# First feed-forward chunk of each layer in two halves of rows, with the first norm and the p projection interleaved

## Chip, cores and metric

One core of a Trainium2 chip runs the whole program in one launch. The metric is the device time of that core in microseconds; the kernel before has a median of 2168.04 us over 3 runs (2167.68 to 2173.33).

## What is computed

The reference is a stack of two blocks over 256 positions of width 1024, in float32. The first block (two layers with attention, memory attention and a gated scan) is not touched. The second has four layers, and each is, cut to what matters:

```python
for i in range(DEPTH_2):                       # 4 layers
    h = mixer_i(x)                             # gla, mla, conv, gla; ends in a product with w_out
    x = layer_norm(ALPHA * x + h, ln_g[i, 0], ln_b[i, 0])                       # first norm
    x = layer_norm(ALPHA * x + sq_relu_mlp(x, mlp_w1[i], mlp_w2[i]), ln_g[i, 1], ln_b[i, 1])
    x = x + jax.nn.sigmoid(x @ ple_w_gate[i]) * (p[i] @ ple_w_proj[i])
```

The feed-forward part squares relu(x @ w1), with w1 of 1024 x 4096, and multiplies with w2, 4096 x 1024. Its hidden width goes in 8 chunks of 512. The projection p @ ple_w_proj (256 x 1024) needs nothing of x.

## The kernel before, in words

`plan()` writes out one list of steps by hand, and every engine walks that same list in order, taking from each step its own part and meeting the others at semaphores. So the list's order is each engine's own order of work.

Weights come as units of 128 x 2048 floats (1 MB), numbered in order of use. SP loads unit n into slot n % 4 of `raw` once the low part of unit n - 4 is made (L746 to L751). ScalarE makes the high part `whi` (`hi`, L1125 to L1130) once the unit that held that slot is done with, told by `unit_begun`; the rest `wlo = raw - whi` is made by VectorE (`lo`, L1427 to L1430) or, for the feed-forward units, by GpSimd (L757 to L767). The step `ahead` and the flag `ahead` of a step say where in the list this is done, three units ahead for ScalarE and two for VectorE. Activations are split in the same way, into `XTh`, `XTl` for X and `YTh`, `YTl` for Y, after being turned (transposed) by TensorE in tiles of 128 x 128; a step `turn` takes 128 rows (h) and 512 columns (c): four transposes (L959), ScalarE's copy to the high part (L1245), VectorE's subtraction for the low part (L1882). Each product is three matmuls, high by high, high by low and low by high (`passes`, L786 to L794, the matmul on L789).

`wait_turned` (L776) makes TensorE wait until what was turned into X or Y is there; a turn marked late counts only for a step that asks for the whole. A turn of p goes to "E", a part of the Y buffers, and L965 and L966 let it count for Y too.

Around the change a layer goes (L441 to L470): the product with w_out in two single units and a tail of two (`output_pair`, which finishes the four quarters, 128 rows by 512 columns each, one after the other), with p turned ahead of the tail. Then the p projection in two halves of columns (`lattm`, 12 matmuls of 512 columns in each half). Then the first norm, `ln` steps on VectorE (L2050 to L2100): for each quarter the sum with the residual (L2057) and statistics (L2061), after two quarters of the same rows the "rest": mean and variance, the normalising products (L2079), an inverse square root by three Newton steps (L2090, L2093), gain and bias into `xres` (L2098). Then the turns of X, rows 0 to 127 first, and chunk 0 of the feed-forward part in two units (u), 512 rows of w1 each. There and in all of `project_unit` in this form the weights are stationary and 256 positions stream: `o` covers all 256 columns of half a bank. The step `mlp` does the other chunks in a loop; its first is chunk 1 (L1104). GpSimd makes the low parts of all 32 feed-forward units of a layer in a loop, each as soon as its high part is there.

Of the kernel before, what the change touches and what calls it, by code (L numbers as in the profile page):

```python
# [24 lines left out]
P = 128  # L25
# [22 lines left out]
def plan():  # L48
# [21 lines left out]
    def add(step, **f):  # L70
        steps.append((step, f))
# [49 lines left out]
    def flush():  # L121
        while late:
            late.pop(0)()
# [97 lines left out]
    def layer_norm(g, early):  # L221

        for c in range(2):
            add("ln", g=g, h=0, part=c)
        add("ln", g=g, h=0, part="rest")
        add("ln", g=g, h=1, part=0)
        if early:
            for c in range(2):
                turn("x", 0, c, "X", 4 * c)
        add("ln", g=g, h=1, part=1)  # L230
        add("ln", g=g, h=1, part="rest")
        if not early:
            for c in range(2):
                turn("x", 0, c, "X", 4 * c)

# [196 lines left out]
    for i in range(LAYERS2):  # L432
# [12 lines left out]
        for b in range(2):  # L445
            if b == 0:
                unit("lattm", (("ple_w_proj", i), "K", 0, 0), g=pg, b=0, k=8)
            else:
                add("lattm", n=len(units) - 1, g=pg + 1, b=1, k=8)
            add("post", g=pg + b, tag="ple", b=b, on="sv")  # L450
        if i == 2:
            add("load", what="gla1")
        layer_norm(q, early=False)
        turn("x", 1, 0, "X", 0)
        turn("x", 1, 1, "X", 4, late=True)
        n0, g = len(units), n["p"]
        unit("proj", ("mlp1", i, 0, 0), g=g, u=0, src="X", fm=True)
        flush()
        add("loadln", i=i, k=1)
        unit("proj", ("mlp1", i, 1, 0), g=g, u=1, src="X", fm=True)  # L460
        add("mlp", i=i, n=n0, g=g, q=n["q"])
        for c in range(1, FF_CHUNKS):
# [140 lines left out]
def build(nc, a, steps, units, heads, totals):  # L603
    NU = len(units)
    with ExitStack() as ctx:
# [151 lines left out]
        @block.gpsimd  # L757
        def _(pool):
            def lo(n, slot):
                pool.wait_ge(hi_done, n + 1)  # L760
                pool.tensor_tensor(wlo[:, slot, :], raw[:, slot, :], whi[:, slot, :],  # L761
                                   ALU.subtract).then_inc(lo_pool, 1)

            for first in (f["n"] for kind, f in steps if kind == "mlp"):
                with pool.Fori(0, 4 * FF_CHUNKS // RING) as i:
                    for s in range(RING):
                        lo(i * RING + (first + s), (first + s) % RING)  # L767
# [3 lines left out]
        def _(pe):  # L771
# [24 lines left out]
            def project_unit(n, slot, g, u, fm, XH=XTh, XL=XTl, KH=4, kx=0, pool_less=None):  # L796
# [8 lines left out]
                for b in range(2):  # L805
# [17 lines left out]
                    elif u == 1:  # L823
                        mm.then_inc(p_done[1], 1)
                return mm

            def output_pair(n, slot, work, XH, XL, k0, first=False):
# [104 lines left out]
            for kind, f in steps:  # L932
                if kind == "turn":
# [29 lines left out]
                    else:  # L963
                        ready[f["dst"]] = f["t"] + 1
                    if f["dst"] == "E":  # L965
                        ready["Y"] = f["t"] + 1  # L966
                elif kind == "proj":
                    wait_turned("Y" if f["src"] == "M" else "X", whole=f["u"] == 1)
                    xs = (YTh, YTl) if f["src"] == "M" else (XTh, XTl)
                    project_unit(f["n"], f["n"] % RING, f["g"], f["u"], f["fm"], *xs)  # L970
                elif kind == "out":
                    wait_turned("Y" if f["src"] == "Y" else "X", whole=False)
# [93 lines left out]
                elif kind in ("latfm", "lattm"):  # L1066
                    wait_turned("Y")
                    wait_lo(pe, f["n"])
# [47 lines left out]
        def _(act):  # L1116
# [96 lines left out]
            for kind, f in steps:  # L1213
# [46 lines left out]
                elif kind in ("latfm", "lattm"):  # L1260
                    if f["b"] == 0:
                        ahead(f["n"])
# [155 lines left out]
        def _(dve):  # L1418
# [393 lines left out]
            for kind, f in steps:  # L1812
# [60 lines left out]
                elif kind in ("latfm", "lattm"):  # L1873
                    if f["b"] == 0:
                        ahead(f["n"])
# [287 lines left out]
```

## Time and profile before

| | |
|---|---|
| median of 3 runs | 2168.04 us |
| the profiled execution | 2167.73 us, of it the span 2165.9 us |
| TensorE busy | 1956.8 us (90%) in 11184 matmuls |
| VectorE busy | 1255.8 us (58%) |
| ScalarE busy | 903.6 us (42%) |
| GpSimd busy | 592.2 us (27%) in 132 instructions |
| DMA | 324.95 MB, mean 150 GB/s |
| mean granted clock of TensorE | 0.962 of 2.4 GHz |

Engines are PE (TensorE matmul), PEld (its weight loads, which overlap), DVE (VectorE), ACT (ScalarE), POOL (GpSimd) and SP. Matmuls are pipelined, so one's duration holds a latency and the pace of a run of them is read from their starts. "L789" is a line of the kernel. A row's bracket says how long the engine was idle ahead of it and who ended that.

### The profile page before, as it was taken

Reading aid. Unit: us, or ns where it says so; the run is one execution under the profiler, and the core shown is the slowest. Engines: PE = TensorE matmul, PEld = TensorE weight load, DVE = VectorE, ACT = ScalarE, POOL = GpSimd, SP = SyncE. Lnnn points to the kernel's source line nnn. Section 1 sums busy time; section 2 is a strip of 40 time slices with the busy share of each in tenths; the row PEclk is TensorE's granted clock in tenths of the full one; section 3 lists DMA queues with packets and bytes.
Section 4 is the critical chain, followed back from the end, with each engine's and each line's share of the span. In section 5 each row is a group of like instructions: output and inputs, shape, how many; then the busy total and the mean of one; then the engine's idle time right before and its main releaser. Section 6 shows DMA issues by size and latency. Waiting matters only on the chain.

```text
span 2165.9 us, 27617 instructions
## 1 busy us (share of the span) xinstructions
PE 1956.8 (90%) x11184; PEld 1710.1 (79%) x11184; DVE 1255.8 (58%) x2094; ACT 903.6 (42%) x969; POOL 592.2 (27%) x132
## 2 busy tenths in 40 slices
PE   6999999899988888999977899989899989879998
PEld 4878877678876776899765699979799977769996
DVE  7777787776876487332764533265732375873235
ACT  4544444345342333344343344434344434334442
POOL 0000000000000002678100378700278700027870
PEclk9999999999899999999999899989999999989999
DMA  6434333533232224455431445534545533254551
GB/s 260 159 127 156 138 135 124 202 146 127 79 136 99 101 94 160 164 187 194 165 117 39 163 174 195 183 142 177 191 166 194 194 117 136 78 180 175 185 195 47
DMA packets 53109, 324.95 MB, mean 150 GB/s; under 512 B 8432, under 2 KB 11888, under 8 KB 15760
## 3 DMA queue, kind: packets, MB, share of 16 engines
q1 hardware_dynamic: 43024, 308.38, 38.6%
q10 hardware_dynamic: 9984, 15.17, 2.2%
q8 instruction: 71, 1.16, 0.2%
q14 instruction: 30, 0.25, 0.0%
HBM read 322.47 MB, written 1.05 MB: 149 GB/s over the span
## 4 chain that ended last, share of the span: by engine, by line
PE 68%; DVE 25%; ACT 3%; issue 3%; DMA 1%; SPq 0%; DVEq 0%; ACTq 0%
PE project L789 37%; PE output L789 24%; DVE wlo L1430 4%; DVE tok L2079 2%; DVE arena L1533 1%; DVE arena L1801 1%; DVE XTl L1882 1%; PE turn L959 1%; PE output L904 1%; PE output L926 1%; DVE xres L2098 1%; DVE st L2061 1%; DVE tok L2057 1%; ACT whi L1130 1%; DVE st L1524 1%
## 5 line engine op out<-in xcount | busy, mean ns | idle before, releaser
L761 POOL TENSOR_TENSOR wlo<-raw,whi 128x2048 fp32r<-128x2048 f32 x128 | 592.0, 4651 | 1524.6 <-ACT whi L1130 1524.2
L1130 ACT ACTIVATE whi<-raw 128x2048 fp32r<-128x2048 f32 x291 | 554.3, 1913 | 511.8 <-PE project L789 311.5
L789 PE MATMUL project<-XTh,whi 128*128 128x256 f32 x1488 | 429.5, 289 | 9.7 <-DVE XTl L1882 8.7
L789 PE MATMUL project<-XTh,wlo 128*128 128x256 f32 x1488 | 427.2, 287 | 0.0
L789 PE MATMUL project<-XTl,whi 128*128 128x256 f32 x1488 | 426.9, 287 | 0.0
L1430 DVE TENSOR_TENSOR wlo<-raw,whi 128x2048 fp32r<-128x2048 f32 x163 | 376.2, 2321 | 66.6 <-ACT whi L1130 66.3
L2107 DVE TENSOR_TENSOR arena<-arena 128x512 f32<-128x512 f32 x64 | 142.4, 2259 | 463.1 <-ACT arena L1380 463.1
L789 PE MATMUL output<-whi,YTh 128*128 128x512 f32 x736 | 293.3, 398 | 21.1 <-DVE YTl L1882 16.7
L789 PEld LDWEIGHTS project<-XTh,whi 128*128 128x128 f32 x1488 | 292.3, 196 | 13.7 <-DVE XTl L1882 11.5
L789 PEld LDWEIGHTS project<-XTh,wlo 128*128 128x128 f32 x1488 | 292.2, 196 | 1.0
L789 PEld LDWEIGHTS project<-XTl,whi 128*128 128x128 f32 x1488 | 291.9, 196 | 0.0
L789 PE MATMUL output<-wlo,YTh 128*128 128x512 f32 x736 | 291.1, 396 | 0.0
L789 PE MATMUL output<-whi,YTl 128*128 128x512 f32 x736 | 290.5, 395 | 0.0
L789 PE MATMUL project<-whi,XTh 128*128 128x512 f32 x624 | 256.6, 411 | 14.4 <-DVE XTl L1882 8.8
L789 PE MATMUL project<-wlo,XTh 128*128 128x512 f32 x624 | 246.6, 395 | 0.0
L789 PE MATMUL project<-whi,XTl 128*128 128x512 f32 x624 | 246.2, 395 | 0.0
L789 PEld LDWEIGHTS output<-whi,YTh 128*128 128x128 f32 x736 | 141.3, 192 | 52.3 <-DVE YTl L1882 18.3
L789 PEld LDWEIGHTS output<-whi,YTl 128*128 128x128 f32 x736 | 140.8, 191 | 30.3
L789 PEld LDWEIGHTS output<-wlo,YTh 128*128 128x128 f32 x736 | 141.1, 192 | 28.0
L789 PEld LDWEIGHTS project<-whi,XTh 128*128 128x128 f32 x624 | 119.7, 192 | 42.2 <-DVE XTl L1882 9.7
L789 PEld LDWEIGHTS project<-whi,XTl 128*128 128x128 f32 x624 | 119.3, 191 | 26.2
L789 PEld LDWEIGHTS project<-wlo,XTh 128*128 128x128 f32 x624 | 119.7, 192 | 23.7
(225 smaller groups left out, 2187.6 us busy)
## 6 DMA issues: line engine op xcount, KB each, us to landing
raw<-in_units SPq DMA_DIRECT2D x291, 1024.0 KB, 4.8
arena<-in_ln_g ACTq DMA_DIRECT2D x8, 512.0 KB, 3.9
arena<-in_ln_b ACTq DMA_DIRECT2D x8, 512.0 KB, 4.8
tok<-in_mem SPq DMA_DIRECT2D x2, 512.0 KB, 5.9
arena<-in_mem_norm_gain ACTq DMA_DIRECT2D x2, 512.0 KB, 4.9
arena<-in_norm_gain ACTq DMA_DIRECT2D x2, 512.0 KB, 5.5
xres<-in_x SPq DMA_DIRECT2D x1, 1024.0 KB, 14.9
arena<-in_mem ACTq DMA_DIRECT2D x1, 1024.0 KB, 7.3
```

The costliest lines, as they stand in the source:

```text
L761: pool.tensor_tensor(wlo[:, slot, :], raw[:, slot, :], whi[:, slot, :], ALU.subtract).then_inc(lo_pool, 1)
L789: mm = pe.matmul(out, x if x_stationary else w, w if x_stationary else x, start=start and i == 0, stop=stop and i == 2, skip_group_check=True)
L904: mm = pe.matmul(PQ[h2][:, h * S:(h + 1) * S], qkT[:, h2, h * P:(h + 1) * P], qkT[:, h2, S:2 * S], start=True, stop=True)
L926: mm = pe.matmul(PQ[3][:, h * P:(h + 1) * P], pT[:, h2, kt * S + h * P:kt * S + (h + 1) * P], v, start=kt == 0, stop=kt == 1)
L959: mm = pe.transpose(PT[f["t"] % 2][:, x * P:(x + 1) * P], s, ident[:, :])
L1130: act.activation(whi[:, slot, :], raw[:, slot, :], ACT.Copy).then_inc(hi_done, 1)
L1430: dve.tensor_tensor(wlo[:, slot, :], raw[:, slot, :], whi[:, slot, :], ALU.subtract).then_inc(lo_dve, 1)
L1524: dve.tensor_reduce(st[:, 16 + 4 * b:20 + 4 * b], sq[:, b, :].rearrange("p (j d) -> p j d", j=4), AX_X, ALU.add).then_inc(dve_own, 1)
L1533: ins = dve.scalar_tensor_tensor(out=v, in0=v, scalar=st[:, 24 + x:25 + x], in1=gain, op0=ALU.mult, op1=ALU.mult)
L1801: ins = dve.copy_predicated(dst, m, src)
L2079: first = [lambda c=c: dve.scalar_tensor_tensor(out=tok[:, h, c * 512:(c + 1) * 512], in0=tok[:, h, c * 512:(c + 1) * 512], scalar=mean, i ...
L2107: dve.tensor_tensor(hsq[:, b, :], relu[:, b, :], relu[:, b, :], ALU.mult).then_inc(hsq_ready, 1)
```

## The change

Around the first norm, the p projection's first half stays ahead of the norm's steps; the turns of rows 0 to 127 come before the second half, and the rest of the norm of rows 128 to 255 comes behind it in the list. A turn into "E" no longer counts for Y, and the p projection waits for "E". Chunk 0 is no longer two `proj` steps but two `first` steps, with new code (`first_chunk`): step h=0 multiplies both units with positions 0 to 127, then rows 128 to 255 are turned, and step h=1 multiplies the same two units with positions 128 to 255. GpSimd's loop has its first four units written out, the third of which waits until the first norm has written all of `xres`. The high parts of the third feed-forward unit and the fourth are made later in the list.

```diff
--- before.py
+++ after.py
@@ -224,14 +224,13 @@
             add("ln", g=g, h=0, part=c)
         add("ln", g=g, h=0, part="rest")
         add("ln", g=g, h=1, part=0)
+        if not early:
+            add("ln", g=g, h=1, part=1)
+        for c in range(2):
+            turn("x", 0, c, "X", 4 * c)
         if early:
-            for c in range(2):
-                turn("x", 0, c, "X", 4 * c)
-        add("ln", g=g, h=1, part=1)
-        add("ln", g=g, h=1, part="rest")
-        if not early:
-            for c in range(2):
-                turn("x", 0, c, "X", 4 * c)
+            add("ln", g=g, h=1, part=1)
+            add("ln", g=g, h=1, part="rest")
 
     def quad(kind, vg, j0=0, **f):
         q = n["quad"]
@@ -444,21 +443,25 @@
         n["p"] += 2
         for b in range(2):
             if b == 0:
-                unit("lattm", (("ple_w_proj", i), "K", 0, 0), g=pg, b=0, k=8)
+                unit("lattm", (("ple_w_proj", i), "K", 0, 0), ahead=False, g=pg, b=0, k=8)
             else:
-                add("lattm", n=len(units) - 1, g=pg + 1, b=1, k=8)
+                layer_norm(q, early=False)
+                add("lattm", n=len(units) - 1, g=pg + 1, b=1, k=8, ahead=False)
             add("post", g=pg + b, tag="ple", b=b, on="sv")
+        add("ln", g=q, h=1, part="rest")
+        add("ahead", n=len(units) - 1)
         if i == 2:
             add("load", what="gla1")
-        layer_norm(q, early=False)
+        n0, g = len(units), n["p"]
+        units.extend(("mlp1", i, u, 0) for u in range(2))
+        add("first", n=n0, g=g, h=0)
+        add("ahead", n=n0)
         turn("x", 1, 0, "X", 0)
-        turn("x", 1, 1, "X", 4, late=True)
-        n0, g = len(units), n["p"]
-        unit("proj", ("mlp1", i, 0, 0), g=g, u=0, src="X", fm=True)
-        flush()
+        turn("x", 1, 1, "X", 4)
         add("loadln", i=i, k=1)
-        unit("proj", ("mlp1", i, 1, 0), g=g, u=1, src="X", fm=True)
-        add("mlp", i=i, n=n0, g=g, q=n["q"])
+        add("first", n=n0, g=g, h=1)
+        add("ahead", n=n0 + 1)
+        add("mlp", i=i, n=n0, g=g, q=n["q"], src_n=n["src"])
         for c in range(1, FF_CHUNKS):
             units.extend(("mlp1", i, u, c) for u in range(2))
             units.extend(("mlp2", i, u, c - 1) for u in range(2))
@@ -761,8 +764,12 @@
                 pool.tensor_tensor(wlo[:, slot, :], raw[:, slot, :], whi[:, slot, :],
                                    ALU.subtract).then_inc(lo_pool, 1)
 
-            for first in (f["n"] for kind, f in steps if kind == "mlp"):
-                with pool.Fori(0, 4 * FF_CHUNKS // RING) as i:
+            for first, normed in ((f["n"], f["src_n"]) for kind, f in steps if kind == "mlp"):
+                for s in range(RING):
+                    if s == 2:
+                        pool.wait_ge(tsrc, normed)
+                    lo(first + s, (first + s) % RING)
+                with pool.Fori(1, 4 * FF_CHUNKS // RING) as i:
                     for s in range(RING):
                         lo(i * RING + (first + s), (first + s) % RING)
 
@@ -823,6 +830,28 @@
                     elif u == 1:
                         mm.then_inc(p_done[1], 1)
                 return mm
+
+            def first_chunk(n, g, h):
+
+                t = slice(h * P, (h + 1) * P)
+                for u in range(2):
+                    slot = (n + u) % RING
+                    if h == 0:
+                        wait_lo(pe, n + u)
+                    begin[0] = u == h
+                    wh = whi[:, slot, :].rearrange("p (k c) -> p k c", k=4)
+                    wl = wlo[:, slot, :].rearrange("p (k c) -> p k c", k=4)
+                    for b in range(2):
+                        if h == 0 and u == 0:
+                            pe.wait_ge(p_evac[b], g)
+                        for m in (2 * b, 2 * b + 1):
+                            o = PP[b][:, (m % 2) * S + h * P:(m % 2) * S + (h + 1) * P]
+                            for k in range(4):
+                                mm = passes(o, XTh[:, 4 * u + k, t], XTl[:, 4 * u + k, t], wh[:, k, m * P:(m + 1) * P],
+                                            wl[:, k, m * P:(m + 1) * P], h == 0 and u == 0 and k == 0 and m % 2 == 0,
+                                            h == 1 and u == 1 and k == 3, x_stationary=False)
+                        if h == 1 and u == 1:
+                            mm.then_inc(p_done[b], 1)
 
             def output_pair(n, slot, work, XH, XL, k0, first=False):
 
@@ -962,12 +991,13 @@
                         late[f["dst"]] = f["t"] + 1
                     else:
                         ready[f["dst"]] = f["t"] + 1
-                    if f["dst"] == "E":
-                        ready["Y"] = f["t"] + 1
                 elif kind == "proj":
                     wait_turned("Y" if f["src"] == "M" else "X", whole=f["u"] == 1)
                     xs = (YTh, YTl) if f["src"] == "M" else (XTh, XTl)
                     project_unit(f["n"], f["n"] % RING, f["g"], f["u"], f["fm"], *xs)
+                elif kind == "first":
+                    wait_turned("X")
+                    first_chunk(f["n"], f["g"], f["h"])
                 elif kind == "out":
                     wait_turned("Y" if f["src"] == "Y" else "X", whole=False)
                     xs = (YTh, YTl) if f["src"] == "Y" else (XTh, XTl)
@@ -1064,7 +1094,7 @@
                                         wl[:, k, b * P:(b + 1) * P], k == 0, k == 7, x_stationary=False)
                         mm.then_inc(p_done[b], 1)
                 elif kind in ("latfm", "lattm"):
-                    wait_turned("Y")
+                    wait_turned("E" if units[f["n"]][0][0] == "ple_w_proj" else "Y")
                     wait_lo(pe, f["n"])
                     begin[0] = f["b"] == 0
                     wh = whi[:, f["n"] % RING, :].rearrange("p (k c) -> p k c", k=2)
@@ -1258,7 +1288,7 @@
                     if f["work"][0][1] == 0:
                         ahead(f["n"] + f["h"])
                 elif kind in ("latfm", "lattm"):
-                    if f["b"] == 0:
+                    if f["b"] == 0 and f["ahead"]:
                         ahead(f["n"])
                 elif kind == "post":
                     if "s" in f["on"]:
@@ -1871,7 +1901,7 @@
                     if f["work"][0][1] == 0:
                         ahead(f["n"] + f["h"])
                 elif kind in ("latfm", "lattm"):
-                    if f["b"] == 0:
+                    if f["b"] == 0 and f["ahead"]:
                         ahead(f["n"])
                 elif kind == "turn":
                     t = f["t"]
```

## Rows read from the trace of the kernel before

**Rows 1.** The page, busy time of one engine and the chain by engine.
```profile
PE 1956.8 (90%) x11184; PEld 1710.1 (79%) x11184; DVE 1255.8 (58%) x2094; ACT 903.6 (42%) x969; POOL 592.2 (27%) x132
...
PE 68%; DVE 25%; ACT 3%; issue 3%; DMA 1%; SPq 0%; DVEq 0%; ACTq 0%
```

**Rows 2.** The chain of waits, 840 to 900 us: start, us, what.
```profile
859.20 7.04 DVE tok L2079 x2
...
869.85 1.10 PE turn L959 x4
...
871.61 0.70 DVE XTl L1882
...
872.35 25.61 PE project L789 x192
```

**Rows 3.** The chain of waits over the whole span, its longest pieces.
```profile
897.97 10.91 PE output L789 x48
908.87 11.51 PE project L789 x96
...
1236.18 24.73 PE project L789 x192
...
1566.69 24.98 PE project L789 x192
...
1947.60 25.59 PE project L789 x192
```

**Rows 4.** Windows: stretch, us, each engine's busy us (instructions), granted clock, DMA share, GB/s.
```profile
855.05:861.49 6.44, 5.85 (x27) 4.53 (x26) 6.27 (x11) 4.42 (x5) 5.32 (x2) 1.00 0.04 17
861.49:872.35 10.86, 2.82 (x17) 2.21 (x14) 9.26 (x13) 2.70 (x5) 4.21 (x1) 0.77 0.53 193
872.35:886.46 14.11, 14.11 (x98) 14.11 (x99) 2.85 (x2) 4.50 (x4) 8.13 (x2) 0.81 0.42 150
```

**Rows 5.** Timeline of PE: start, us, instruction, [idle before <- releaser].
```profile
844.05 0.47 PE L789 MATMUL output<-whi,YTh 128*128 128x512 f32 x1 [1.09 <-DVE YTl L1882]
...
858.52 0.47 PE L789 MATMUL project<-whi,YTh 128*128 128x512 f32 x1 [0.59 <-ACT arena L1139]
...
861.34 1.03 PE L959 MATMUL turn<-ident,xres 128*128 128x128 f32 x8
...
1225.17 1.03 PE L959 MATMUL turn<-ident,xres 128*128 128x128 f32 x8
...
1555.67 1.03 PE L959 MATMUL turn<-ident,xres 128*128 128x128 f32 x8
...
1936.62 1.03 PE L959 MATMUL turn<-ident,xres 128*128 128x128 f32 x8
```

**Rows 6.** Timeline of the other engines in the first layer's stretch.
```profile
843.87 2.28 DVE L1430 TENSOR_TENSOR wlo<-raw,whi 128x2048 fp32r<-128x2048 f32 x1
...
851.75 1.42 DVE L2079 SCALAR_TENSOR_TENSOR tok<-tok,st,arena 128x512 f32<-128x512 f32 x2
...
854.62 1.42 DVE L2098 SCALAR_TENSOR_TENSOR xres<-tok,st,arena 128x512 f32<-128x512 f32 x2
...
856.17 9.52 POOL L761 TENSOR_TENSOR wlo<-raw,whi 128x2048 fp32r<-128x2048 f32 x2 [4.96 <-ACT whi L1130]
...
862.03 1.08 ACT L1245 ACTIVATE XTh<-turn 128x512 fp32r<-128x512 f32 x2
```

**Rows 7.** Groups of weight loads by shape (count, busy us, mean ns), and two pieces of PE's timeline.
```profile
L789 PEld LDWEIGHTS project<-XTh,whi 128*128 128x128 f32 x1488 | 292.3, 196 | 13.7 <-DVE XTl L1882 11.5 <-DVE wlo L1430 1.2
...
L926 PEld LDWEIGHTS output<-arena 128*128 128x128 f32 x256 | 32.1, 191 | 5.8 <-DVE arena L1708 4.7
...
L1046 PEld LDWEIGHTS project<-XTl,arena 128*16 128x16 f32 x32 | 3.1, 97 | 3.8
...
134.77 1.06 PE L926 MATMUL output<-arena 128*128 128x128 f32 x8
...
566.35 2.05 PE L1015 MATMUL output<-arena 128*128 128x128 f32 x16 [0.34 <-DVE arena L1760]
```

## The prediction

> **What bounds the kernel now.** I read the page first: the tensor engine is busy for 90% of the span, and the chain that ended last lies on it for 68% and on the vector engine for 25% [rows 1]. So matmul work moves the time one for one, and so do the places where it waits for the vector engine. The change touches one place, four times: from the tail of a layer's output product, over the first norm, to the first two feed-forward chunks. The chain of waits around it in the first layer [rows 2] shows what to see: after the tail the path leaves the tensor engine for the norm; in the second half's norm two instructions take 7.04 us; then come transposes, one more low part of XT, and 25.61 us of first-layer products. Inside the loop the same 96 products take 11.51 us and 48 of 512 columns take 10.91 us [rows 3]: 119.9 ns and 227.3 ns apart. The 192 products of chunks 0 and 1 should then take 23.02 us; they took 25.61, 24.73, 24.98 and 25.59 us [rows 2, 3]. The windows say why: from 861.49 to 872.35 the tensor engine was busy 2.82 of 10.86 us, and the next 14.11 us ran at a granted clock of 0.81, a mix of 1.2 and 2.4 GHz [rows 4]. The timeline gives the points I count from [rows 5].
>
> **Part 1, the tail no longer waits for the turned p.** In before a turn into "E" also raises what "Y" stands for, so the tail, which reads only Y, waits for p's low part: 1.09 us, ahead of the tail [rows 5], and alike in all four layers. The change takes that line out and lets only the p projection wait. The low part needed next, for the tail's second unit, was made long before; and the tail's end sets the norm's start. Each layer gains 1.09 us. The VectorE subtraction that stood behind p's turn ends at 846.15 [rows 6], about when the tail's first quarter now ends, so some 0.1 us may come back; I leave it out.
>
> **Part 2, the norm and the p projection change places.** The first half of the projection stays ahead; the two turns of rows 0 to 127 and then the second half follow. The turns cost 8 transposes at 0.11 us, 0.9 us (8 took 1.03 with the last one's 0.27 latency [rows 5]), where PE stood 0.59 us waiting for ScalarE's copy (the idle time at 858.52 [rows 5]). That copy was late since ScalarE made two high parts in front of it; one is now deferred. So the second projection ends 0.9 - 0.59, less what was already overlapped, about 0.15 us later; I take 861.40 for the start of the first half-chunk in the old time, against 861.34 for the old turns [rows 5]. Is its input ready? The norm of rows 0 to 127 ends at 854.62 + 1.42 = 856.04 [rows 6], the statistics of the other rows at 859.2, where L2079 began [rows 2]. ScalarE's two copies take 1.08 us [rows 6], the two low parts 0.70 each [rows 2], so XT's first half is whole at about 860.5: in time by 0.9 us, hidden behind the second projection. Without that cover PE would stand from 858.7 to 860.5, 1.8 us.
>
> **Part 3, the stall of the second norm.** L2079 takes 1.42 us for two in the first half's norm [rows 6] and 7.04 us in the second's [rows 2]. GpSimd's low parts of the weights run 856.17 to 865.69 [rows 6], and the pair ended just after: both read two tensors from SBUF. The change holds the third low part back until the norm has written all its rows. The first of these two ends at 860.8, about where the rest of the norm now begins (it stands behind the two low parts of XT), so the norm of rows 128 to 255 should take from its L2079 on what the first took, 851.75 to 856.04 [rows 6]: it ends near 865.1, before the first half-chunk ends. So it leaves the path altogether; even with the whole 5.6 us stall it would end at 870.7, still before about 872.7. What is late next is no norm but the products. Held back: the third low part (about 865.2 to 869.8) and the fourth (to 874.4); they are used at about 887. SP's loads behind them and ScalarE's high parts move with them and have the same slack. The fifth and sixth weight units wait for the unit two before to be begun, about 1 us later than now, and are used after 898. LN constants and the third layer's small loads are issued beside products. All that at nothing.
>
> **Part 4, 96 products of 256 columns become 192 of 128.** Stationary are the weights, so every product needs its own weight load, and those double. No such product is in the trace, so I bound it. From below by columns alone: (227.3 - 119.9) / 256 is 0.42 ns a column, so 119.9 - 53.7 = 66 ns, if the load hides. From above, while loads and clock behave as now, by the 256-column product's 119.9. What the load asks is in the groups of weight loads [rows 7]: loads of 128 columns take 191 (plain fp32) and 196 ns (these), one of 16 takes 97; that is 0.84 ns a column, 107 ns for 128. Two loops of plain fp32 with such loads and 128 columns run 8 in 1.06 us and 16 in 2.05 us; less one latency of 0.28 that is 111 and 118 ns each. So the load, not the columns, should set the pace, and halving the columns saves nearly nothing: I take 118, nearest to the longer of the loops and just under the 119.9 of the same instruction.
>
> The skill has another figure. The Trainium skill ("TensorE: Matmul & The Clock Gate", Back-to-back issue gap) gives a sustained stream of loads and matmuls about 81 ns at 128 columns. By it the 192 products would take an estimated 15.6 us, and the sum would come to some 7 us less a layer. That figure's operands are not these; whether it holds here is the second rival's question.
>
> Between the halves stand two turns. The old ones show their cost: begun 861.34, copied by 863.11 [rows 5, 6], plus one low part of 0.70 [rows 2]: 2.5 us in which PE does 0.9 us of transposes.
>
> **Sum per layer**, from the old turns' start to the end of chunk 1. Before: 36.62, 35.74, 36.00 and 36.57 us (872.35 + 25.61 - 861.34, and so on [rows 2, 3, 5]), mean 36.23. After: 0.06 + 192 x 0.118 + 2.5 + 11.51 for chunk 1 + 0.17 latency = 36.90. That is +0.67, less 1.09 from part 1: -0.42 us; over four layers -1.7 us. With 111 to 120 ns it is -7.1 to -0.2 us. The profiled execution took 2167.73 us (span 2165.9 and 1.8 around), 0.3 under the median of 2168.04; I put the same difference on the median: 2166.3 us.
>
> **Rivals.** One, the clock falls in the pause between the halves. Before, the half-rate stretch behind the norm cost 2.6, 1.7, 2.0 and 2.6 us (above 23.02), 8.8 in all; my sum holds none of it. PE idled 7.5 us at a stretch then and would idle some 1.6 now, and the pause at 858.52 left the clock at 1.00 [rows 4], so I think it stays; if not, -1.7 + 8.8 gives 2175 us. Chance 0.08.
> Two, the weight load hides in the reordering and 128 columns cost 66 ns: 12.7 instead of 22.7 us, 10 us a layer, 2126 us (the norm still ends in time). For it: nothing shows a load setting the pace alone. Against it: the 0.84 ns a column. The skill's figure named above lies between. Chance 0.07.
> Three, on the other side, and with one mechanism: products this narrow lose the one-column-a-cycle rate. A plain fp32 product is two instructions of 111 to 118 ns, so 0.23 us each; if 128 columns of this type run at that rate, the half-chunks take 44.2 us, +21.5 a layer, 2252 us. It decides from about 0.13 us a product on. The same 192 at 1.2 GHz throughout (loads of 213 ns, twice 107) would give 2239. Against: the loads in the 256-column loop show the load time alone explains a floor there. Chance 0.13 for both.
> That the change doesn't do what it says (the stall stays) costs nothing, as part 3 showed, so it is no case of its own.
>
> **How the numbers follow.** The forecast has 0.72. About 0.3%, 6.5 us, is what a measurement of this kernel can tell from no change. Its bounds of -7.1 to -0.2 and about 1 us a layer of doubt on the pause make it 0.14 faster, 0.56 same, 0.02 slower; rival one adds 0.06 slower and 0.02 same; rival two 0.07 faster; rival three 0.13 slower. Sum: 0.21, 0.58, 0.21. The range takes the forecast with its bounds (2157) and rival one (2178 with the same doubt), 0.8 together.
>
> **What the profile after would show.** Tail without the 1.09 us wait; L2079 at 1.42 us for two in both halves; 96 products of 128 columns in 11.3 us twice, 2.5 us apart, from about 860.3 on; their granted clock 1.0; chunk 1 ending within a microsecond of 897. Wrong it would be made by products under 0.1 or over 0.13 us apart, by a clock of 0.5 after the pause, or by a weight unit arriving late at chunk 1.

## The result and the profile after

The changed kernel takes 2196.24 us in the median of 4 runs (2192.84 to 2202.01), the kernel before 2167.97 in runs beside it: the ratio is 1.0136, with an interval of 1.011 to 1.0162. It is slower by some 28 us, and outside the range of the prediction.

The page of the changed kernel: span, busy time by engine, and the chain by engine.

```profile
span 2194.5 us, 28359 instructions
...
PE 2017.6 (92%) x11568; PEld 1774.7 (81%) x11568; DVE 1219.1 (56%) x2094; ACT 903.4 (41%) x969; POOL 591.3 (27%) x132
...
PE 72%; DVE 21%; ACT 3%; issue 2%; DMA 1%; SPq 0%; DVEq 0%; ACTq 0%
```

VectorE's share of the chain fell from 25% [rows 1] to 21%, as it should with the norm out of the way, and TensorE's rose from 68% to 72% of a longer span. The 384 added matmuls are the 96 a layer that the split adds; TensorE's busy time grew by 61 us.

The chain of waits over the whole span, after; the pieces that answer to [rows 2, 3]. A piece of 108 is the last 12 products of the p projection and the first half-chunk of 96; a piece of 192 is the second half-chunk and chunk 1.

```profile
853.00 13.41 PE project L796 x108
...
868.97 33.67 PE project L796 x192
902.64 10.91 PE output L796 x48
913.55 11.51 PE project L796 x96
...
1243.84 32.14 PE project L796 x192
...
1581.02 32.08 PE project L796 x192
...
1968.13 33.68 PE project L796 x192
```

The first half is what was hoped for: 13.41 less 2.72 for the 12 wide products is 10.69 us for 96, 111 ns each. The second half is the same 96 products on other rows, and with chunk 1's 11.5 us it should take some 22.2 us. It takes 32.1 to 33.7, in all four layers. The windows of the first layer show where (stretch, us, busy us and count of each engine, granted clock, DMA share, GB/s):

```profile
861.00:866.25 5.25, 5.25 (x50) 5.25 (x49) 0.00 (x0) 0.00 (x0) 5.25 (x2) 1.00 0.26 78
866.25:868.97 2.72, 1.05 (x10) 0.85 (x10) 1.29 (x2) 1.08 (x2) 1.96 (x1) 1.00 0.75 291
868.97:873.00 4.03, 4.03 (x23) 4.03 (x23) 0.00 (x0) 0.00 (x0) 0.00 (x0) 0.60 1.03 345
873.00:878.00 5.00, 5.00 (x25) 5.00 (x25) 0.00 (x0) 0.00 (x0) 0.00 (x0) 0.50 0.28 115
878.00:888.78 10.78, 10.78 (x53) 10.78 (x52) 1.51 (x1) 2.51 (x2) 4.52 (x1) 0.50 0.20 61
888.78:891.00 2.22, 2.22 (x11) 2.22 (x12) 1.29 (x2) 1.75 (x4) 0.00 (x0) 0.50 0.42 177
891.00:894.00 3.00, 3.00 (x18) 3.00 (x17) 0.69 (x1) 1.80 (x2) 1.12 (x1) 0.56 0.00 0
894.00:902.64 8.64, 8.64 (x74) 8.64 (x73) 2.21 (x1) 2.51 (x2) 7.04 (x2) 1.00 0.33 123
```

The clock is 1.0 through the first half and through the pause, 2.72 us in which TensorE is busy 1.05 and idle 1.67. It falls to 1.2 GHz just after the second half has begun, stays there to its end, and comes back only inside chunk 1, which begins at 888.78 and whose products have 256 columns: 4.9 us into it here, and 2.6, 4.0 and 4.7 us in the other layers. TensorE's timeline shows the moment: products 0.11 us apart, then 0.21.

```profile
869.44 0.28 PE L796 MATMUL project<-XTh,wlo 128*128 128x128 f32 x1
869.55 0.28 PE L796 MATMUL project<-XTl,whi 128*128 128x128 f32 x1
869.66 0.33 PE L796 MATMUL project<-XTh,whi 128*128 128x128 f32 x1
869.79 0.42 PE L796 MATMUL project<-XTh,wlo 128*128 128x128 f32 x1
870.00 0.41 PE L796 MATMUL project<-XTl,whi 128*128 128x128 f32 x1
```

The norm did what was predicted. VectorE's and GpSimd's timeline:

```profile
854.80 1.42 DVE L2109 SCALAR_TENSOR_TENSOR tok<-tok,st,arena 128x512 f32<-128x512 f32 x2
...
850.37 4.62 POOL L764 TENSOR_TENSOR wlo<-raw,whi 128x2048 fp32r<-128x2048 f32 x1 [4.21 <-ACT whi L1160]
859.15 9.07 POOL L764 TENSOR_TENSOR wlo<-raw,whi 128x2048 fp32r<-128x2048 f32 x2 [4.17 <-DVE xres L2128]
```

The pair that took 7.04 us [rows 2] takes 1.42, and GpSimd's third low part starts when the norm has written its last rows.

**The account.** From the tail's first product to the end of chunk 1, by the chain, the four layers took 53.92, 53.03, 53.29 and 53.91 us before and take 64.15, 62.62, 62.60 and 64.20: 39.4 more in all. The low clock is 33.67 - 22.48 = 11.2 us in two layers and 9.6 in the other two, 41.6 together (22.48 is what the piece of 192 takes at full clock in the fifth run below; in the sixth it is 22.24). The rest is the prediction's own +2.7, less 5.0 for a pace of 111 in place of 118 ns. Outside this stretch the tail's shorter wait gives 4.4 back, and 6.4 more, which is what is then left of the difference of the spans, went in stretches that the change doesn't touch: in one the clock happened to be 0.86 before,

```profile
615.00:640.00 25.00, 18.87 (x85) 15.66 (x84) 22.89 (x35) 12.46 (x11) 0.00 (x0) 0.86 0.35 126
```

and 1.00 in the same work after:

```profile
613.00:638.00 25.00, 18.88 (x96) 15.46 (x97) 24.22 (x35) 14.39 (x12) 0.00 (x0) 1.00 0.34 126
```

39.4 - 4.4 - 6.4 = 28.6, the difference of the spans. Outside the four stretches the trace before has 126 us at 1.2 GHz and the one after 112, and at half rate 14 us of it cost about 7 (an estimate), enough for the 6.4.

### The profile page after: what moved, and what is told of

Same layout as the page of the kernel before. It is cut to its first block, busy times and chain, and to the rows that moved or that the text cites. A ratio compares the mean times of both kernels' runs of the same rounds, so it can differ in the third digit from the quotient of the medians.

```text
span 2194.5 us, 28359 instructions
## 1 busy us (share of the span) xinstructions
PE 2017.6 (92%) x11568; PEld 1774.7 (81%) x11568; DVE 1219.1 (56%) x2094; ACT 903.4 (41%) x969; POOL 591.3 (27%) x132
## 3 DMA queue, kind: packets, MB, share of 16 engines
HBM read 322.47 MB, written 1.05 MB: 147 GB/s over the span
## 4 chain that ended last, share of the span: by engine, by line
PE 72%; DVE 21%; ACT 3%; issue 2%; DMA 1%; SPq 0%; DVEq 0%; ACTq 0%
PE project L796 41%; PE output L796 24%; DVE wlo L1460 4%; DVE arena L1563 1%; DVE arena L1831 1%; PE turn L988 1%; DVE XTl L1912 1%; PE output L933 1%; PE output L955 1%; ACT whi L1160 1%; DVE st L1554 1%; DVE arena L1725 1%; PE project L1076 1%; DVE arena L1783 1%; DVE arena L1785 1%
## 5 line engine op out<-in xcount | busy, mean ns | idle before, releaser
L796 PE MATMUL project<-XTh,whi 128*128 128x256 f32 (+1 forms) x1616 | 477.2, 295 | 14.5 <-DVE XTl L1912 13.1
L796 PE MATMUL project<-XTh,wlo 128*128 128x256 f32 (+1 forms) x1616 | 475.8, 294 | 0.0
L796 PE MATMUL project<-XTl,whi 128*128 128x256 f32 (+1 forms) x1616 | 475.7, 294 | 0.0
L2137 DVE TENSOR_TENSOR arena<-arena 128x512 f32<-128x512 f32 x64 | 129.3, 2054 | 510.6 <-ACT arena L1410 510.6
L796 PEld LDWEIGHTS project<-XTh,whi 128*128 128x128 f32 x1616 | 330.9, 205 | 17.8 <-DVE XTl L1912 15.1
L796 PEld LDWEIGHTS project<-XTh,wlo 128*128 128x128 f32 x1616 | 331.1, 205 | 1.2
L796 PEld LDWEIGHTS project<-XTl,whi 128*128 128x128 f32 x1616 | 330.9, 205 | 0.0
```

The costliest lines, as they stand in the source:

```text
L796: mm = pe.matmul(out, x if x_stationary else w, w if x_stationary else x, start=start and i == 0, stop=stop and i == 2, skip_group_check=True)
L2137: dve.tensor_tensor(hsq[:, b, :], relu[:, b, :], relu[:, b, :], ALU.mult).then_inc(hsq_ready, 1)
```

## The experiments

The question left by the traces is what brings the clock down and keeps it down: the pause between the halves, or the narrow products themselves. "Pieces" below are those of the chain that hold chunk 1.

A median holds more than the change. The work ahead of the first layer's turn of p is the same in all these kernels, yet in their profiled executions that turn begins anywhere from 834.95 us (run 1) to 850.26 us (run 7), with 41 to 68 us at 1.2 GHz ahead of it. What such differences don't touch is the stretch from p's turn to the end of chunk 1, summed over the four layers: 220.9 us before and 256.0 in the changed kernel. It is given below where it says more than the median.

**1. No pause.** The turns go between the two units of the first half, and the second of these units doesn't wait for them (that part of the edit is left out here).

```diff
-        add("first", n=n0, g=g, h=0)
+        add("first", n=n0, g=g, h=0, us=(0,))
         add("ahead", n=n0)
         turn("x", 1, 0, "X", 0)
         turn("x", 1, 1, "X", 4)
         add("loadln", i=i, k=1)
-        add("first", n=n0, g=g, h=1)
+        add("first", n=n0, g=g, h=0, us=(1,))
+        add("first", n=n0, g=g, h=1, us=(0, 1))
```

> The turns of rows 128 to 255 are issued between the two units of the first half-chunk, so TensorE has no pause between the halves; all products of the changed kernel are kept. Pause theory (the idle 1.7 us brought the clock down): no fall, both halves at 0.111 us a product, from the first narrow product to the end of chunk 1 about 34 us in place of 46 to 47, near 2147 us. Narrow theory (128-column products do not hold the full clock by themselves): the clock still falls, 10 to 15 us after the first narrow product, and stays low until chunk 1; only the 1.7 us of idling go, near 2189 us.

Measured: 2150.7 us (2139.3 to 2158.5, 6 runs), ratio to the kernel before 0.9928 (0.9907 to 0.9949). In the profiled execution, of 2139.3 us, the clock fell in none of the four layers. The chain (240 are 144 narrow products and chunk 1):

```profile
859.05 27.59 PE project L797 x240
...
1217.62 27.59 PE project L797 x240
```

144 at 111 ns and 11.5 us make 27.5. So 21 us of narrow products, with nothing but the turns in between, did not lower the clock here. The other runs are 11 to 19 us longer, about what one fall or two cost, but they need none: the stretch is 206.7 us, 14.2 less than before, which puts the median near 2154, and 2150.7 was measured. The profiled execution was the fortunate one: it spent 95 us at 1.2 GHz outside its four stretches where the kernel before spent 126. The other five have a mean clock of 0.969 to 0.974 in place of 0.978, so more of them was at 1.2 GHz; where in the program was not recorded.

**2. Narrow products alone.** The kernel before, its norm and order, with `first_chunk` in place of the two units, both halves back to back (the function is that of the changed kernel and is left out here).

```diff
-        unit("proj", ("mlp1", i, 0, 0), g=g, u=0, src="X", fm=True)
         flush()
+        units.extend(("mlp1", i, u, 0) for u in range(2))
+        add("first", n=n0, g=g, h=0)
+        add("ahead", n=n0)
         add("loadln", i=i, k=1)
-        unit("proj", ("mlp1", i, 1, 0), g=g, u=1, src="X", fm=True)
+        add("first", n=n0, g=g, h=1)
+        add("ahead", n=n0 + 1)
```

> The kernel before with its norm, order and waits, and chunk 0 in 192 products of 128 columns back to back, without a pause, begun after the old 7.5 us pause at half clock. Narrow theory: the 192 never bring the clock up: 41 us, chunk 1 about 14 us, some 30 us a layer more than before, near 2287 us. Pause theory: the clock comes back after about 3 us and the 192 take some 23 us, 9 us a layer more, near 2205 us.

Measured: 2290.04 us, ratio 1.0571 (1.0534 to 1.0607). The chain, and the windows:

```profile
871.32 54.62 PE project L792 x288
```

```profile
871.32:912.20 40.88, 40.88 (x192) 40.88 (x192) 1.53 (x1) 4.42 (x3) 9.05 (x2) 0.50 0.21 68
912.20:925.90 13.70, 13.70 (x99) 13.70 (x99) 4.15 (x4) 6.07 (x6) 8.11 (x2) 0.84 0.27 106
```

Begun at 1.2 GHz, 192 narrow products never left it, in 41 us; the wide ones of chunk 1 brought it up within their 13.7 us, at a mean of 0.84, after 4.2 to 5.1 us in the four layers. That is the narrow theory's number. Together with run 1: in these two profiled executions narrow products without a gap kept the clock that they found.

**3 to 5. What must lie on either side of the pause.** In run 3 unit 0 goes ahead of the pause and unit 1 behind it, both with 256 columns:

```diff
-                    first_chunk(f["n"], f["g"], f["h"])
+                    project_unit(f["n"] + f["h"], (f["n"] + f["h"]) % RING, f["g"], f["h"], True)
```

> Unit 0 as 48 products of 256 columns ahead of the pause, unit 1 as 48 behind it, the turns and the pause as in the changed kernel. Left out: rows 128 to 255 of X are stale for unit 0. Pause theory: the clock falls shortly after the pause here too, and comes back within a few us. Narrow theory: granted clock 1.0 on both sides, 0.12 us a product, both units 5.8 us.

In run 4 the first half stays, and 96 products of 256 columns stand behind the pause; in run 5 it is the other way round. The products are those of `project_unit` for both units:

```diff
-                    first_chunk(f["n"], f["g"], f["h"])
+                    if f["h"] == 0:      # run 5: == 1
+                        first_chunk(f["n"], f["g"], f["h"])
+                    else:
+                        for u in range(2):
...
+                                        mm = passes(o, XTh[:, 4 * u + k, :], XTl[:, 4 * u + k, :],
```

> First half as in the changed kernel (96 products of 128 columns), the pause, then 96 products of 256 columns in place of the second half's 96 of 128. Changed in what is computed: positions 0 to 127 are added twice. Pause theory and narrow theory both let the clock fall behind the pause; the narrow theory says that wide products bring it back within about 3 us (the 96 take 13 to 14 us in place of 20), the pause theory alone says the same as for narrow ones. If the clock does not fall at all, it takes narrow products after the pause, too.

> Ahead of the pause 96 products of 256 columns in place of 96 of 128, behind it the 96 of 128 as in the changed kernel. Changed in what is computed: the first step also adds stale rows 128 to 255. If it takes narrow products on both sides of the pause: the clock stays at 1.0, the second half 10.7 us. If narrow products behind a pause are enough: it falls again and the half takes some 20 us. The earlier run with narrow ahead and wide behind did not fall.

Measured in one run each: 2113.93, 2155.71 and 2184.47 us. These totals don't compare, since the three don't do the same products (run 3 has 96 in chunk 0 and runs 4 and 5 have 192, half of them wide, and each takes some rows stale or twice); the chain does. That of run 3 (48 products and chunk 1), of which one layer of four equal ones is shown:

```profile
864.33 17.51 PE project L796 x144
```

of run 4 (96 wide and chunk 1), likewise:

```profile
866.22 23.27 PE project L796 x192
```

and of run 5 (96 narrow and chunk 1):

```profile
874.50 22.48 PE project L796 x192
...
1239.21 33.67 PE project L796 x192
...
1577.22 33.67 PE project L796 x192
...
1967.50 22.48 PE project L796 x192
```

With wide products behind the same pause (2.5 us from 861.84 to 864.33 in run 3) the clock did not fall in any layer, whatever stood ahead of it: 144 x 0.12 is 17.3 and 192 x 0.12 is 23.0. With narrow ones behind and wide ones ahead it fell in two layers of four. My expectation had only all or nothing here. With narrow on both sides, the changed kernel, it fell in four of four. Why the same products behind the same pause lose the clock in two layers and keep it in two is not shown.

Wide products don't hold the clock behind every wait. Further on in the changed kernel 48 products of 256 columns stand behind waits of 1.1 and 1.4 us with four transposes between them, and the clock fell 0.9 us after the first:

```profile
1466.18 7.51 PE project L796 x48
```

Where the clock stays, such a piece takes 6.0 us.

**6. The pause filled.** Nine products of 512 columns in the pause, results thrown away.

```diff
+                    if f["h"] == 1:
+                        for x in range(9):
+                            pe.matmul(PQ[x % 2][:, :], XTh[:, x % 4, 0:P], whi[:, f["n"] % RING, 0:512],
+                                      start=True, stop=True, skip_group_check=True)
                     wait_turned("X")
```

> The changed kernel with nine extra products of 512 columns issued in the pause between the halves (2.0 us of work into banks of no use then); their results are thrown away. If idling inside a stretch of narrow products is what brings the clock down: it stays at 1.0, the second half takes 10.7 us in place of 18 to 20, near 2150 us. If narrow products behind any interruption bring it down: it falls as in the changed kernel, near 2197 us.

Measured: 2161.53 us in one run, and in all four layers a piece of 22.24:

```profile
872.52 22.24 PE project L796 x192
```

Work that serves nothing, 2 us a layer of it, takes some 35 us off the changed kernel (one run against the median of four), and 41 off the stretch. Expected was 2150 us, 46 less: 5 of the missing 11 lie in the stretch and 6 outside, where this execution has 128 us at 1.2 GHz and the changed kernel's 112. With products of 128 columns the idling is needed for the fall, in all that was run here.

**7. A shorter pause.** The last turn is marked late, and only unit 1 of the second half waits for it (the change of the wait is left out here). TensorE idles 0.98 us between the halves.

```diff
-        turn("x", 1, 1, "X", 4)
+        turn("x", 1, 1, "X", 4, late=True)
```

> The changed kernel with the last turn marked late, so the second half's unit 0 starts without the low part that only unit 1 needs: TensorE idles about 1.0 us between the halves in place of 1.7. If the length of the pause decides: no fall, both halves 10.7 us, near 2150 us. If any pause in narrow products will do: the clock falls in all four layers, near 2193 us. In between, with falls in some layers, 11 us for each.

Measured: 2175.52 us (2166.52 to 2186.89, 10 runs), ratio 1.0029 (1.0007 to 1.005). In the profiled execution two layers fell and two did not:

```profile
880.65 22.49 PE project L796 x192
...
1245.01 32.08 PE project L796 x192
```

The wide spread of the runs fits a number of falls that differs from run to run.

**8. Fewer columns, no pause.** Run 1 with every narrow product streaming 64 columns.

```diff
-                t = slice(h * P, (h + 1) * P)
+                t = slice(h * P, h * P + 64)
...
-                            o = PP[b][:, (m % 2) * S + h * P:(m % 2) * S + (h + 1) * P]
+                            o = PP[b][:, (m % 2) * S + h * P:(m % 2) * S + h * P + 64]
```

> The run with the turns inside, each narrow product streaming 64 columns in place of 128 (positions 64 to 127 and 192 to 255 of chunk 0 are left out). If the weight load sets the pace of a narrow product: still 0.111 us a product, 16.1 us for the 144 after the turns. If the streamed columns do: 0.083 us or less, 12 us or less. Of the clock: the array streams half as much, so if that is what the chip looks at, the clock falls here without any pause.

Measured: 2224.2 us in one run. TensorE's timeline:

```profile
865.73 0.28 PE L797 MATMUL project<-XTl,whi 128*128 128x64 f32 x1
865.85 0.29 PE L797 MATMUL project<-XTh,whi 128*128 128x64 f32 x1
865.96 0.40 PE L797 MATMUL project<-XTh,wlo 128*128 128x64 f32 x1
866.17 0.40 PE L797 MATMUL project<-XTl,whi 128*128 128x64 f32 x1
```

and the windows:

```profile
862.00:864.50 2.50, 2.50 (x25) 2.50 (x24) 2.25 (x9) 2.39 (x3) 0.00 (x0) 1.00 0.83 262
...
870.27:901.00 30.73, 30.73 (x146) 30.73 (x145) 2.71 (x3) 3.24 (x4) 8.76 (x2) 0.50 0.36 129
```

Two answers. At full clock the pace is still 0.11 us a product with half the columns, so the columns don't set it. What else a product has is its weight load of 128 columns, and the prediction's estimate of 107 ns for that fits. And the clock falls some 4 us after the first such product with no pause at all, in all four layers (pieces of 43.4 to 44.6). To the row's measure "busy" the engine is busy throughout, 2.50 of 2.50 us. What separates this run from run 1 is the 64 columns in place of 128 in each product. (Half of chunk 0's positions are left out, so the kernel's result is not the reference's.)

**9. The order without the split.** Chunk 0 as two units of 256 columns once X is whole.

```diff
-        add("first", n=n0, g=g, h=0)
-        add("ahead", n=n0)
         turn("x", 1, 0, "X", 0)
         turn("x", 1, 1, "X", 4)
         add("loadln", i=i, k=1)
-        add("first", n=n0, g=g, h=1)
-        add("ahead", n=n0 + 1)
+        for u in range(2):
+            add("proj", n=n0 + u, ahead=True, g=g, u=u, src="X", fm=True)
```

> The change without its part 4: the new order around the norm, the shorter wait of the tail and the held-back low parts stay, chunk 0 is two units of 256-column products begun when all of X is turned. PE then stands some 5 us for the second norm and its turns, and begins about 6 us behind the end of the projection. With the clock kept: 23.0 us for chunks 0 and 1, near 2125 us. With a fall as in the kernel before: about 2 us a layer more, near 2134 us. Either way the new order alone gains some 35 to 43 us on the kernel before, and the split gives that away.

Measured: 2146.56 us (2138.93 to 2148.93, 4 runs), ratio 0.9897 (0.987 to 0.9924). The expected gain was right in sign and too large by 12 to 21 us. The stretch gained 26.0 us (194.9 in place of 220.9), and the profiled execution came to the first turn of p 7 us later than the one before the change, with 10 us more at 1.2 GHz ahead of it; 8 us of the 34 that were expected with a fall are missing from the stretch itself, and why stays open. TensorE waits for the norm and its turns, and the clock falls, but the 96 wide products bring it back:

```profile
872.92 25.52 PE project L794 x192
```

2.5 us above 23.0, as before the change [rows 2]. So the new order alone gains some 21 us, and the split turns that into a loss of 28. Not all of that is the fall: run 1, which has the split and no fall, has a stretch of 206.7 us, 12 above this run's. The split is dearer than the waits that it fills even with the clock kept.

**10. Without holding GpSimd back.** Run 9, with the third low part made as early as before.

```diff
-                    if s == 2:
-                        pool.wait_ge(tsrc, normed)
...
-        add("ahead", n=len(units) - 1)
...
-                unit("lattm", (("ple_w_proj", i), "K", 0, 0), ahead=False, g=pg, b=0, k=8)
+                unit("lattm", (("ple_w_proj", i), "K", 0, 0), g=pg, b=0, k=8)
...
-                add("lattm", n=len(units) - 1, g=pg + 1, b=1, k=8, ahead=False)
+                add("lattm", n=len(units) - 1, g=pg + 1, b=1, k=8)
```

> The run with the order alone, less the held-back low part (GpSimd makes its third low part as soon as ScalarE's high part is there, and that is made ahead of the norm again). If the stall of the second norm is GpSimd's doing: L2079's pair takes up to 7 us again, chunk 0 begins some 5 us a layer later, near 2166 us. Rival: the new order has moved the pair past GpSimd's work, and the time stays near 2146 us.

Measured: 2162.72 us (10 runs), ratio 0.9979 (0.9961 to 0.9997): 16 us above run 9, 4 a layer. The timeline has the stall back, two instructions in 5.58 us beside GpSimd's pair:

```profile
852.30 5.58 DVE L2104 SCALAR_TENSOR_TENSOR tok<-tok,st,arena 128x512 f32<-128x512 f32 x2
```

It is the same in all four layers. 5.58 - 1.42 is 4.2 us a layer, which is the 16. GpSimd's pair runs from 847.57 to 856.67, and the first of the two VectorE instructions, begun at 852.30, ends at 857.22, just behind it. The Trainium skill ("SBUF — State Buffer", Who interferes with whom) says that a VectorE instruction with two inputs in SBUF contends with a GpSimd instruction that reads SBUF, for a port pair that is an exclusive lock. These rows agree.

**11. The tail's wait alone**, in the kernel before.

```diff
-                    if f["dst"] == "E":
-                        ready["Y"] = f["t"] + 1
```

(and the p projection waits for "E".)

> The kernel before with part 1 alone: the tail of a layer's output product no longer waits for the turned p. Prediction's term: 1.09 us a layer, 4.4 us in all, near 2163.7 us; the wait behind p's turn gone from the profile. Rival: the norm's start hangs on the subtraction that VectorE does ahead of it, so that less than 1 us a layer is kept, down to nothing.

Measured: 2165.71 us (12 runs), ratio 0.9985 (0.9968 to 1.0001). The wait of [rows 5] is gone: the tail starts 0.35 us behind p's turn in place of 1.69.

```profile
843.05 0.60 PE L959 MATMUL turn<-ident,arena 128*128 128x128 f32 x4
843.40 0.48 PE L789 MATMUL output<-whi,YTh 128*128 128x512 f32 x1
```

The median moved by 2.3 us. The interval, 6.9 us faster to 0.2 slower, holds the 4.4 of the prediction and a half of it, so the total is not settled by it. The trace settles what reaches the products: from p's turn to the first product of chunk 0 the four layers took 29.99, 29.98, 29.98 and 29.99 us before and take 28.67, 28.65, 28.66 and 28.67, so 1.3 us a layer is kept, and the rival is out.

**12. A version that beats both.** Only unit 0 in halves of rows, with the turns inside the first half's products; unit 1 with 256 columns. (The rewritten `first_chunk` is left out here.)

```diff
+        add("first", n=n0, g=g, h=0, ms=(0, 1, 2))
+        add("ahead", n=n0)
         turn("x", 1, 0, "X", 0)
         turn("x", 1, 1, "X", 4)
         add("loadln", i=i, k=1)
+        add("first", n=n0, g=g, h=0, ms=(3,))
+        add("first", n=n0, g=g, h=1, ms=(0, 1, 2, 3))
+        add("proj", n=n0 + 1, ahead=True, g=g, u=1, src="X", fm=True)
```

> Only unit 0 of chunk 0 in two halves of rows (96 products of 128 columns), with the turns of rows 128 to 255 inside the first half's products, unit 1 in 48 products of 256 columns. If narrow products keep the full clock as long as nothing stands still: 10.7 + 0.9 + 5.8 + 11.5 us from the first product to the end of chunk 1, some 29.5 with a short wait for the low part, near 2124 us, equal to or a few us under the order alone. If the short wait inside it brings the clock down: some 10 us a layer more.

Measured: 2138.61 us (2131.04 to 2144.52, 4 runs), ratio 0.9859 (0.9834 to 0.9884): 29 us faster than the kernel before and 58 faster than the changed one, 8 faster than the order alone, and 15 slower than expected. Its stretch is 189.1 us, 31.8 less than before. The 96 narrow products cover the norm but for 0.4 us, which TensorE waits at 872.20 with narrow products on both sides, and no layer loses the clock (48 narrow, 48 wide and chunk 1):

```profile
872.57 22.88 PE project L797 x192
```

## Why the prediction was wrong

**Part 1, the tail.** The wait is gone from the trace, as said. Its 4.4 us lie within the interval of run 11, which does not pin them down; in run 11's trace 1.3 us a layer reach chunk 0.

**Part 2, the order.** Right: XT's first half was ready in time, the first half-chunk followed the projection without a wait.

**Part 3, the stall.** Right in cause and in size at its place (7.04 to 1.42 us), and run 10 shows what it is worth where the norm is on the path: 4 us a layer. In the changed kernel the second norm ends at 859.07, 7 us ahead of need.

**Part 4, the narrow products.** Right in the main: halving the columns saves nearly nothing, and run 8, which halves them again at the same pace, shows that they don't set it. The size was a little off: 111 ns where I took 118. That the shorter of the two plain loops has the same 111 is in part luck, for those loops can't show a load's pace. The kernel before has plain fp32 products of 256 columns with loads of only 16, 32 instructions for 16 products:

```profile
732.05 7.08 PE project L1046 x32
```

They are 216 ns apart, so plain fp32 takes 0.84 ns a column by streaming alone, and 128 columns of it some 108 ns (an estimate from this row) whatever their load takes. The better ground was the loads' own 107 ns. Rival two (66 ns) and rival three (two passes, 230 ns) fall with that, and so does the 81 ns of the Trainium skill ("TensorE: Matmul & The Clock Gate", Back-to-back issue gap) for operands like these.

**The step that failed** is rival one: "the clock falls in the pause between the halves", priced at 8.8 us over four layers with a chance of 0.08. The mechanism was there, and both its numbers were wrong. The sum held nothing for it, and it came in every layer. The price came from the kernel before, where the products that follow the pause have 256 columns and bring the clock back within 3.3 to 5.3 us. I moved that price to products of 128 columns without asking whether they bring it back. They don't (run 2), so the fall lasts for the whole second half and into chunk 1: 9.6 to 11.2 us a layer, 41.6 in all, nearly five times the price. The chance leaned on a pause in the old trace that left the clock alone, at 858.52, in work of 512 columns and only 0.59 us long. Runs 3 to 5 show that the products behind the pause matter: behind the new pause wide ones held the clock and narrow ones lost it in two layers or four of four. Run 7 shows that its length may: at 1.0 us in place of 1.7 two layers of four kept the clock. Which of the two spared the old pause is not shown. My case of 1.2 GHz "throughout", in rival three, had the right price per product (213 ns) but no trigger, when the trigger stood two rivals above it. The two belonged together.

With 10.4 us a layer for that, and 111 for 118 ns, the prediction's own sum gives -1.7 + 41.6 - 5.0, some 35 us; the spans differ by 28.6, and the other 6.4 are clock differences elsewhere that come and go.

What stays open: how often the clock falls in run 1 and run 7 outside the profiled executions, and why, with narrow products behind the pause, it falls in some layers and not in others (runs 5 and 7).

## What to carry to other kernels

Cutting products in two to fill a wait doubles their weight loads; where a load of 128 columns already takes about as long as 256 columns of streaming (an estimated 107 ns each), a half costs nearly as much as a whole, 111 ns against 120, and the wait that is filled must be worth that. In these traces such narrow work kept a full clock through 21 us without a gap and through a wait of 0.4 us, lost it behind a pause of 1.0 or 1.7 us in half of the layers or in all, and did not bring a low clock back in 41 us. So put no pause inside or ahead of it, place what it waits for inside its own stream, and return to wide products soon. A price for "the clock falls" must be taken from the same shape of products as will follow the fall. And when two versions differ by less than some 15 us, compare the stretch that was changed: the first 840 us of this program, the same in all runs, varied by that much.

## What the runs showed of the hardware

- Products of 128 columns of this type run 111 ns apart at full clock and 213 ns apart at 1.2 GHz; with 64 columns they run at the same 111 ns.
- 192 of 128 columns, begun at 1.2 GHz, stayed there for 41 us without a gap (run 2); chunk 1's 256-column products left it after 4.2 to 5.1 us there, and after 2.6 to 4.9 us in the changed kernel. With 64 columns the clock fell without a pause, some 4 us after the first (run 8).
- An idle 1.7 us with narrow products on both sides was followed by a fall in four layers of four (the changed kernel); about 1.0 us in two of four (run 7); 0.4 us in none (run 12); 1.7 us with wide products ahead and narrow behind in two (run 5), with wide behind in none (runs 3 and 4); the 1.7 filled with wide products in none (run 6).
- Plain fp32 products of 256 columns with loads of 16 columns run 216 ns apart at full clock (the kernel before, 732.05 us).
- Two VectorE instructions with two inputs in SBUF, 1.42 us alone, took 7.04 us (before) and 5.58 us (run 10) beside GpSimd's instructions on weights; GpSimd's took 4.5 to 5.0 us each there.
